# Group norms by token columns, with the sums made inside the mixers, in a kernel of five transformer layers

## What is computed

```python
def head_rms_norm(h, w, eps=1e-6):
    hf = h.astype(F32)
    return hf * lax.rsqrt(jnp.mean(hf * hf, -1, keepdims=True) + eps) * w.astype(F32)
...
        h_out = num / jnp.maximum(jnp.abs(den), jnp.exp(-m_t))[..., None]
...
    y = head_rms_norm(hs, norm_w.reshape(A_HEADS, A_DV)) * o
    return y.reshape(bsz, seq, vw).astype(w_out.dtype) @ w_out
```

## Time and profile before

| what | value |
|---|---|
| three runs | 3413.23, 3416.01, 3422.43 us; median 3416.01 |
| profiled execution | 3419.95 us, of which span 3418.1 us |
| TensorE busy | 3291.5 us (96%) |
| VectorE / ScalarE / POOL busy | 1617.6 / 1204.2 / 1468.6 us |
| DMA | 376.06 MB, 110 GB/s over the span |

### The profile page before, as it was taken

One profiled execution on the slowest core, in us unless ns is written; L12 is line 12 of the kernel. 1 busy time (PEld: TensorE's weight loads), 2 busy tenths in 40 slices (PEclk: granted clock), 3 DMA queues, 4 the chain that ended last, 5 costly groups with the idle time before them and its releaser, 6 DMA issues.

```text
span 3418.1 us, 42050 instructions
## 1 busy us (share of the span) xinstructions
PE 3291.5 (96%) x14836; PEld 2602.3 (76%) x14836; DVE 1617.6 (47%) x2690; ACT 1204.2 (35%) x1874; POOL 1468.6 (43%) x715
## 2 busy tenths in 40 slices
PE   7999899999999999999999999999999999899998
PEld 6756578887766888877788878776888887578886
DVE  2254535521236455458655433567555453752223
ACT  3245333322234432246533243114432242543322
POOL 3440154445324544451644445444544464054442
PEclk9979999999999999999999999999999999999999
DMA  4310045542211555320455423112555322023332
GB/s 142 104 50 1 1 146 189 200 154 93 86 55 62 194 188 199 106 89 4 143 192 200 154 80 105 56 32 74 197 188 199 106 89 80 1 80 98 96 100 68
DMA packets 103104, 376.06 MB, mean 110 GB/s; under 512 B 11457, under 2 KB 11585, under 8 KB 102849
## 3 DMA queue, kind: packets, MB, share of 16 engines
q1 hardware_dynamic: 102816, 373.86, 32.8%
q0 software_dynamic: 160, 0.52, 0.1%
HBM read 372.24 MB, written 2.10 MB: 110 GB/s over the span
## 4 chain that ended last, share of the span: by engine, by line
PE 84%; DVE 3%; issue 1%; ACT 1%; POOL 0%; DVEq 0%; ACTq 0%; POOLq 0%
PE bank L689 20%; PE bank L691 20%; PE bank L690 20%; PE bank L780 2%; PE bank L775 2%; PE bank L776 2%; PE bank L1181 2%; PE bank L733 1%; PE bank L735 1%; PE bank L734 1%; PE bank L919 1%; PE bank L899 1%; PE bank L874 1%; PE bank L1088 1%; PE bank L1089 1%
## 5 line engine op out<-in xcount | busy, mean ns | idle before, releaser
L571 POOL TENSOR_TENSOR w_lo<-raw,w_hi 128x1024 fp32r<-128x1024 f32 x501 | 1224.5, 2449 | 1421.8 <-ACT w_hi L1258 1421.8
L1258 ACT ACTIVATE w_hi<-raw 128x1024 fp32r<-128x1024 f32 x501 | 526.8, 1057 | 1217.0 <-PE bank L691 1021.3
L689 PE MATMUL bank<-h_hi,w_hi 128*128 128x512 f32 x2264 | 884.3, 391 | 0.0
L691 PE MATMUL bank<-h_hi,w_lo 128*128 128x512 f32 x2264 | 882.0, 390 | 0.0
L690 PE MATMUL bank<-h_lo,w_hi 128*128 128x512 f32 x2264 | 882.0, 390 | 0.0
L689 PEld LDWEIGHTS bank<-h_hi,w_hi 128*128 128x128 f32 x2264 | 425.6, 188 | 90.4 <-issue 2.6
L690 PEld LDWEIGHTS bank<-h_lo,w_hi 128*128 128x128 f32 x2264 | 425.5, 188 | 88.7 <-issue 1.0
L691 PEld LDWEIGHTS bank<-h_hi,w_lo 128*128 128x128 f32 x2264 | 425.5, 188 | 88.3
L2261 DVE CUSTOM_DVE_ANT_0 ada_raw<-ada_raw,cond_row 128x1024 f32<-128x1024 f32 x192 | 301.4, 1573 | 280.0 <-DMA ada_raw<-ada 271.3
L689 PE MATMUL bank<-hid_hi,w_hi 128*128 128x512 f32 x880 | 344.2, 391 | 0.0
L691 PE MATMUL bank<-hid_hi,w_lo 128*128 128x512 f32 x880 | 342.7, 389 | 0.0
(11 more groups left out here) (356 smaller groups left out, 4100.0 us busy)
## 6 DMA issues: line engine op xcount, KB each, us to landing
raw<-weights SPq DMA_DIRECT2D x501, 512.0 KB, 3.5
ada_raw<-ada SPq DMA_DIRECT2D x192, 512.0 KB, 4.3
layer_const<-layer_const SPq DMA_DIRECT2D x5, 512.0 KB, 3.8
x<-x_t SPq DMA_DIRECT2D x1, 2048.0 KB, 7.5
cond_row<-cond SPq DMA_DIRECT2D x4, 512.0 KB, 4.2
y_t<-x SPq DMA_DIRECT2D x8, 256.0 KB, 2.0
tables<-big_const SPq DMA_DIRECT2D x1, 768.0 KB, 6.5
cols<-columns SPq DMA_DIRECT2D x1, 569.5 KB, 8.5
```

What stands on the lines that cost most here:

```text
L571: nc.gpsimd.tensor_tensor(w_lo[k % RING][:, :, :], raw[k % RING][:, :, :], w_hi[k % RING][:, :, :].bitcast(F32), ALU.subtract).then_inc(sm ...
L689: mm(out, w_hi[r][:, at, :], hi, start=first and at == 0, stop=False)
L691: op = mm(out, w_lo[r][:, at, :], hi, start=False, stop=last and at == len(pairs) - 1)
L1258: fn(w_hi[t % RING][:, :, :], raw[t % RING][:, :, :], ACT.Copy).then_inc(sm.hi_done, 1)
```

## The change

- The sums are made by token columns: the square is the stationary operand (four blocks of 128 tokens), a column of ones (or two half columns, for 64-wide groups) moves. A head's sum is then 4 columns (one per block of tokens), with tokens on the partitions. Root and reciprocal work on a few columns of `small` for several heads at once.
- The spread is four transposes of a column that is broadcast (for 64-wide groups, VectorE first writes out a 128x512 tile `wide`: `group_widen`).
- Squares and sums of heads that are finished are made inside the mixer: seven of eight in the first layer, layer 2 and layer 3, three of four in layer 0. The first root, the reciprocal and two spreads also come before the mixer's end.
- mLSTM: denominators are ten products with one moving column into columns of bank 2, floors are transposed with the other rows, numerators are copied undivided, and the size of the denominator enters the norm (1e-6 times its square is added to the mean square). The sigmoid is taken at each gate's eviction.
- Banks move: differential scores use three banks rather than four, dilated attention three output banks rather than four.

```diff
@@ TensorE
-            def group_sum(items, t):
-
-                it = items[t]
-                for u in range(len(it["src"])):
-                    n.add(gt=1)
-                    pe.wait_ge(sm.g_sq, n["gt"])
-                    rows, at = it["src"][u].shape[0], 32 * (t % 4)
-                    mm(bank[6 + t // 4][at:at + 32, :], it["mat"], sq[(n["gt"] - 1) % 2][0:rows, :], start=u == 0,
-                       stop=u == len(it["src"]) - 1).then_inc(sm.g_sum, 1)
...
+            def group_sum(kind, items, t):
+
+                src, mat = items[t]["src"], items[t]["mat"]
+                out, w = norm_sums(kind, t, t + 1), mat.shape[1]
...
+                pe.wait_ge(sm.g_sq, n["gt"])
+                for k in range(TT):
+                    for u in range(len(src)):
+                        op = mm(out[:, k * w:(k + 1) * w], squares[u][:, k * P:(k + 1) * P], mat, start=u == 0,
+                                stop=u == len(src) - 1)
+                op.then_inc(sm.g_sum, len(src))
...
+                    pe.wait_ge(sm.g_inv, n["gq"] + 1 + (t >= NORM_EARLY[kind]))
+                    for k in range(TT):
+                        c = inverse[:, k * w:k * w + 1].to_broadcast([P, rows])
+                        op = turn(out[0:rows, k * P:(k + 1) * P], c, ident)
+                op.then_inc(sm.g_spread, 1)
...
+            def normed_linear(part, items, summed):
+
+                c, few = 0, len(items) == 4
                 for t in range(len(items)):
-                    group_sum(items, t)
-                for t in range(len(items) + 2):
-                    if t < len(items):
-                        group_spread(part, t, (4, 5))
-                    if t >= 2:
-                        for _ in items[t - 2]["src"]:
-                            early_chunk(c)
-                            c += 1
...
+                    if t == 1:
+                        if few:
+                            pe.wait_ge(sm.ml_dd, 2)
+                        for late in range(summed, len(items)):
+                            group_sum(part, items, late)
+                    if t + 2 < len(items) and not (few and t == 1):
+                        out_spread(part, items, t + 2)
+                    for _ in items[t]["src"]:
+                        early_chunk(c)
+                        c += 1
+                    if few and t == 1:
+                        out_spread(part, items, t + 2)
@@ TensorE, diff_attention
+                    if step >= 10 and step % 4 == 2 and step < len(DF_UNITS):
+                        group_sum(3, items, (step - 10) // 4)
+                    if step == len(DF_UNITS) + 1:
+                        out_spread(3, items, 0)
+                        group_sum(3, items, 6)
@@ TensorE, mlstm
-                    for j in range(TT):
-                        op = mm(bank[6][:, j * P:S], ones, a[:, CO[j]:CO[j] + CW[j]], start=j == 0, stop=j == TT - 1)
+                    for t in range(TT):
+                        for j in range(t + 1):
+                            at = CO[j] + (t - j) * P
+                            op = mm(ml_den[:, 4 * hd + t:4 * hd + t + 1], a[:, at:at + P], one, start=j == 0, stop=j == t)
...
                     if hd < 3:
-                        for g in range(2 * hd + 2, 2 * hd + 4):
-                            gate_piece(g, bank[5][:, :], range(DT))
+                        gate_piece(2 * hd + 2, bank[5][:, :], range(DT))
+                        if hd == 2:
+                            pe.wait_ge(sm.ml_dd, 1)
+                        group_sum(0, items, hd)
+                        gate_piece(2 * hd + 3, bank[5][:, :], range(DT))
@@ TensorE, hgrn
+                    if s - 1 in HG_SQUARE:
+                        group_sum(2, items, HG_SQUARE[s - 1])
@@ TensorE, mlstm_rows
-                elif s == 4:
...
-                    for hd in range(4):
-                        op = mm(bank[(5, 6, 7, 4)[hd]][:, :], lc[0:4, hd * P:(hd + 1) * P], ml_r[0:4, 6, :], start=True,
-                                stop=True)
@@ ScalarE, mlstm
-                    for g in range(2 * hd, 2 * hd + 2):
-                        gate_evicted(g, proj[:, 8 + g, :], bank[5][:, :], ACT.Copy)
+                    if hd:
+                        act.wait_ge(sm.ml_out, 2 * hd)
+                    gate_evicted(2 * hd, proj[:, 8 + 2 * hd, :], bank[5][:, :], ACT.Sigmoid)
+                    if hd:
+                        group_squares(0, items, hd - 1)
+                    gate_evicted(2 * hd + 1, proj[:, 9 + 2 * hd, :], bank[5][:, :], ACT.Sigmoid)
...
+                group_root(0, items, 0)
@@ VectorE, mlstm output
-                    link(v.scalar_tensor_tensor(x_h, bank[6][:, :], -1.0, x_h, ALU.mult, ALU.max))
-                    link(v.scalar_tensor_tensor(ml_t[:, :], bank[6][:, :], 1.0, x_h, ALU.mult, ALU.max))
-                    link(v.reciprocal(ml_t[:, :], ml_t[:, :]))
...
+                        v.tensor_copy(proj[:, 2 * hd + e, :], bank[6 + e][:, :]).then_inc(sm.ml_out, 1)
```

More of the change, by code:

```diff
@@ L347, in program @@
         ml_w = small[:, 0:16]
+        ml_low = small[:, 16:32]
         lb = small[:, 0:8]
@@ new lines, in group_spread @@
+            def group_spread(kind, items, t, out):
+                rows, w = items[t]["src"][0].shape[0], items[t]["mat"].shape[1]
+                inverse = norm_columns(kind, t, t + 1)
+                if widened(items[t]):
+                    n.add(gw=1)
+                    pe.wait_ge(sm.g_wide, n["gw"])
+                    for k in range(TT):
+                        op = turn(out[:, k * P:(k + 1) * P], wide[n["gw"] % 2][:, k * P:(k + 1) * P], ident)
+                else:
+                    pe.wait_ge(sm.g_inv, n["gq"] + 1 + (t >= NORM_EARLY[kind]))
+                    for k in range(TT):
+                        c = inverse[:, k * w:k * w + 1].to_broadcast([P, rows])
+                        op = turn(out[0:rows, k * P:(k + 1) * P], c, ident)
+                op.then_inc(sm.g_spread, 1)
@@ L1185, in hgrn @@
                 values(7)
+                for t in range(2):
+                    out_spread(2, items, t)
             def ffn(sums):
@@ L1860, in group_norm, with group_norms, attention @@
                 op.then_inc(sm.g_out, 1)
-            def group_norms(items):
-                group_inverse(0)
-                for t in range(len(items)):
-                    if t == 2 and len(items) > 4:
-                        group_inverse(1)
-                    group_norm(items, t, (4, 5))
-                n.add(gn=len(items), part=DT)
-            def attention(jobs, bufs):
+            def group_norms(part, items, before=lambda t: None):
+                few = len(items) == 4
+                for t in range(1, len(items)):
+                    before(t)
+                    if t == (3 if few else 4):
+                        group_inverse(part, items, 1)
+                    group_widen(part, items, t + 1)
+                    group_norm(items, t, NORM_SPREAD[part])
+                n.add(gn=len(items), part=DT, gsum=DT)
+            def attention(jobs, bufs, between=lambda step: None, outs=4):
                 a, g = n["att"], n["att_g"]
@@ L2341, in _ @@
                     diff_attention()
-                wait(dve, sm.att_out, n["att_g"])
-                if out_norms(part):
-                    group_norms(out_norms(part))
-                else:
+                if part in ("first", 3):
+                    group_norms(part, out_norms(part))
+                elif part == 1:
+                    dve.wait_ge(sm.att_out, n["att_g"])
                     n.add(part=DT)
```

338 lines of the change are left out of this document (228 added, 110 removed).

## The result

The changed kernel takes **3397.71 us** (median of five runs, 3394.11 to 3403.26), the kernel before 3416.83 us (five runs, 3413.23 to 3422.43). The ratio is 0.9945, 95% interval 0.993 to 0.9959: faster by 19.1 us. Its profiled execution took 3400.3 us, 19.65 less than that of before.

The account below looks back on a forecast made before the run. TensorE, busy 96% of the span, was taken as the bound. Terms summed to -24.5 us from the profiled 3419.95, giving 3395.5; less 3.9 to the median, 3392 us. Forecast range 3382 to 3403 (chance 0.65), 8 in 10 for 3376 to 3409.

Parts of the forecast that it names:

- Layer 0's heads: Three heads in `mlstm`: TensorE waits 4.0 us for squares, then a 1.95 us sum and half clock worth 1.7: +20.8 us.
- rival B's first half: Layer 0's heads: each wait brings about 7 us at half clock, not 3.4, another 5 us; whole rival's chance 0.15.
- Layer 0's end: From the numerators to the last chunk: 45.6 us become 29, VectorE's wide reciprocals gone, -16.6 us.
- Floors: Layer 0: 3.7 us of floor products and 1.7 of slow clock go, for four tiny transposes (0.4): -5.0 us.
- Layer 3: Layer 3's end shrinks from 37.6 to 25 us, gaining 12.6; sums moved into its mixer cost 3.9: -8.7 us.
- two thirds: Layer 3's mixer: six moved sums, 5.9 us in all, are counted at only this share, 3.9 us.
- Layer 2: Layer 2's end shrinks from 38.7 to 26.5 us, gaining 12.2; seven sums in its mixer cost 6.9: -5.5 us.
- rival C: Mixers: the clock falls at each of 20 sums, 1.7 us each, 34 on top; slower, 3434 us; chance 0.04.
- First layer's end: End shrinks from 40.9 to 26.3 us, gaining 14.6; seven sums moved ahead cost 6.9: -7.5 us.
- Queries and keys: Norms of queries and keys: eight spreads, -0.45 us each, less a bit for widened tiles: -2 us.
- rival B's second half: First layer's block projections: clock stays down after every sum and spread, costing 8.5 us; whole rival's chance 0.15.
- The signs: Layer 3's first chunk within 3 us, layer 2's within 5; three 4 us waits; 1 us sums; TensorE idle 25 us less.

Follow-up runs that it names:

- experiment 1: Changed kernel, but in three heads of layer 0 ScalarE squares the finished head before evicting the next gate piece: 3379.31 us, 0.9885 of before.
- experiment 3: Changed kernel, but layer 0's eight gate pieces are evicted by a plain copy, without the sigmoid: 3394.70 us.
- experiment 6: Changed kernel, but each sum of squares of the first layer, layer 2 and layer 3 is computed twice: 3421.95 us.
- experiment 10: Kernel of experiment 1, but layer 2's sums of squares stand at the end of their step instead of its beginning: 3374.78 us in a single execution.
- experiment 8: The kernel before the change, run once more unchanged for a second profile: 3417.10 us.
- experiment 11: Changed kernel with squares ahead of the gate's eviction, row sums inside the gate piece, layer 2's sums at their step's end: 3373.65 us, 0.9864 of before.
- experiment 7: Kernel of experiment 1, but each sum of layer 0 is computed twice: 3391.17 us in a single execution.
- experiment 9: Kernel of experiment 1, but the row sums of heads 0 to 2 stand between the halves of the next gate piece: 3377.03 us, single execution.

## Why the prediction was right, term by term

The time, 3397.71, lies 5.7 us over the forecast of 3392 and inside its range. The main mechanism was the one forecast: the ends behind the mixers shrink, and three waits of 4 us in layer 0's heads take a part back. The sum of the terms was -24.5 us, the profiles differ by -19.65. That the sum is so near is partly luck: the heads of layer 0 and the queries and keys came out 12 us worse than forecast, the other terms and the clock of single stages 8 us better. Two terms were also added up wrongly, layer 2 (12.2 less 6.9 is 5.3, not 5.5) and the first layer's end (14.6 less 6.9 is 7.7, not 7.5); the two slips cancel.

- **Layer 0's heads, +20.8.** Measured to the end of the last head's row sums (1032.4, the end of the group at 1030.11): 113.0 us against 86.0 from `mlstm`'s start to 1019.11: +27.0. This is the term that was mis-sized. The waits are right to the tenth, 12.1 us for 3 x 4.0, and each with the cause named: experiment 1 removes them by order alone, experiment 3 shows the load as 1.3 of each. The clock was taken as one stretch of 3.4 us per head; the profile has 10.2, 6.8 and 10.2 us. The sums themselves run slow (9.5 us for three where experiment 1 has 1.84 each), and then a part of the next gate piece: the 15.5 us at the lower level behind the sums cost 7.7. Waits of 12.1 less the 2.0 that waits for evictions fell by, 9.5 of sums and 7.7 of clock make 27.3. That is rival B's first half, and it came nearly as priced (5 us more). I took the 3.4 us behind the floor products as the size of a drop; it was the smallest there is.
- **Layer 0's end, -16.6**: 28.0 us from there to the end of the last chunk, forecast 29, so -17.6. The spreads' wait for the root was 1.39 us.
- **Floors, -5.0**: -4.8 in their stage.
- **Layer 3, -8.7**: -10.9. The end is 19.9 us from the mixer's last product to the last chunk, where I wrote 25. Of these 25, a sum and two spreads (1.7 us, 2959.55 to 2961.27) stand ahead of the mixer's last product; for the rest spreads cost 0.47 and not 0.65, and the 1.5 us for a table load beside the last copies were not paid. The mixer grew by 6.7 us (2876.8 to 2962.2 against 2886.2 to 2964.9), 5.0 without that sum and those spreads, where I had 3.9: experiment 6 says that "two thirds" was too little, the added sums cost their full length there. Two errors of opposite sign.
- **Layer 2, -5.5**: -5.9, again by two errors: its end shrank by 14.6 us where I had 12.2, its mixer grew by 8.9 where I had 6.9. In the mixer stands one stretch at half clock (6.8 us of it, 3.4 us of time), which I had said would speak for rival C. It comes once and not some 20 times, and it begins 2.0 us ahead of the sum there, behind a wait of 1.85 us that the kernel before has as well, without a drop. So it is not shown that the sum sets it off; experiment 10 takes 3.0 us back by moving the sums.
- **First layer's end, -7.5**: -10.9, but the second profile of before is 3.2 us shorter in this stage, by its clock alone. Against that one the term is -7.7. Here too the end shrank by more than forecast (19.8 us for 14.6, part of it that clock) and the mixer grew by more (8.8 for 6.9).
- **Queries and keys, -2**: +4.2 in the two stages up to the dilated heads. The products did get cheaper, but the clock of 152 to 203 us fell from 0.83 to 0.70, and in this execution stayed down for 24 us behind 218, in the attention, where I had not looked. By experiment 8 it is +4.3 or -2.3, by the place at which the clock falls. The clock of 152 to 203 us is 0.70 to 0.73 in every profile with the change and 0.83 in both of the kernel before, so rival B's second half is true in direction. That the two stages come out longer by it shows in three of nine profiles. The changed kernel's windows there:

```profile
152.00:203.00 51.00, 51.00 (x252) 0.70 0.30 93
218.00:243.00 25.00, 21.77 (x71) 0.52 0.00 0
```

- The other stages: -2.3 at the start, of which 1.7 by the clock near 50 us; this stage took 149.5 to 153.8 us in the profiles with the change. +1.5 in the stages to layer 2's mixer, to layer 3's mixer and to the end.
- **The signs.** The first chunks came 0.4 and 3.8 us behind the mixers' last products, the three waits and the sums of about 1 us are there. One sign failed: TensorE's idle time was to fall by about 25 us at the same busy time; it fell by 8.5 us and the busy time by 11.1, and the other 5 us were not gained.

By the Trainium skill, ScalarE: Activation LUTs, What ACT_TABLE_LOAD costs, a drain of 1380 ns goes with each load. Here 1.28 us of load are followed by the sigmoid 0.02 us later, and a wait without the load is 1.2 to 1.3 us shorter (experiment 3). The trace does not agree, and it decides. The Trainium skill, TensorE: Matmul & The Clock Gate, Part 4 (PE-mode transpose), says that a transpose does not count as busy the way a product does. That could have shown at the ends, where each spread is four of them. The chunks and spreads of 2962 to 2982 us run at 1.00 throughout, with 2.04 us of wide products for each 0.47 us of spread, so here it made no difference.

## What to carry to other kernels

When work of a finished item is moved between the steps of the next one, look on the producing engine at what stands in the queue ahead of it: here the order of two calls on ScalarE cost some 20 us, as much as the whole change had gained. Price a wait on TensorE with the clock around it, and as a range from the shortest to the longest drop that the profile shows, not at the shortest alone: here 5.1 us were forecast for three drops, and they cost 11.7 (4.0 in the sums, 7.7 behind them). Count narrow products at their full length even beside an engine that TensorE waits for in turn, unless a run with twice as many of them says otherwise: in layer 3 the doubled ones cost 0.9 us each.

## What the hardware showed that I had not expected

- A stretch at the lower clock was anything from 3.4 to 23.9 us long. Where it falls is not a property of the code alone: the same instructions have it in one execution and not in the next (3.2 us at the first layer's end in two executions of before, 3.3 us in layer 3 in experiment 11, 6.5 us in the first layer's attention). A difference of some 3 us between two profiles says nothing before the clock of that stage has been compared.
- A drop came without any wait: in experiment 7 while 32 one-column records (3.7 us at full clock) ran in a row, in two of three places. Moving twenty of them (2.29 us) between wide products moved a drop and kept the number of drops (experiment 9).
- A table load ran ahead of the data it is for where the activation behind it had one wait (head 0 and experiment 1); with two, one of them was on the load, and the load waited.
